# Two gate projections in front of the retention core, swapped output banks, and rotary angles between the first splits

## What is computed

```python
def hybrid_layer(x, positions, ...):
    h = rmsnorm(x, norm_mix)
    cb, cc, cu, q, k, v, g, ga, gb = split(h @ w_in)
    y_conv = short_conv_mixer(cb, cc, cu, conv_w, w_conv_out)
    y_ret = retention_mixer(q, k, v, g, positions, ret_norm, w_ret_out)
    merged = sigmoid(ga) * y_conv + sigmoid(gb) * y_ret
    x = x + merged @ w_o
    h2 = rmsnorm(x, norm_mlp)
    return x + square(relu(h2 @ w_up)) @ w_down

# retention_mixer: 4 heads, q and k of 128, v of 256 features each
q, k = rotary(q, positions) * 128 ** -0.5, rotary(k, positions)
o = retention_core(q, k, v)          # sum over earlier tokens, weights decay with distance
o = (o - mean(o)) * rsqrt(var(o) + EPS) * ret_norm       # mean and variance per head
return (silu(g) * o) @ w_ret_out
```

## Time and profile before

| | |
|---|---|
| median of 3 runs | 2580.82 us (2580.22 to 2585.51) |
| the profiled execution: time, span | 2584.02 us, 2582.0 us |
| TensorE busy with matmuls | 2475.8 us, 96% |
| VectorE, GpSimd, ScalarE busy | 51%, 53%, 31% |
| share of the chain that ended last | TensorE 85%, VectorE 8% and its queue 3% |

### The profile page before, as it was taken

One profiled execution on the slowest core, in us unless ns is written; L12 is line 12 of the kernel. 1 busy time (PEld: TensorE's weight loads), 2 busy tenths in 40 slices (PEclk: granted clock), 3 DMA queues, 4 the chain that ended last, 5 costly groups with the idle time before them and its releaser, 6 DMA issues.

```text
span 2582.0 us, 33584 instructions
## 1 busy us (share of the span) xinstructions
PE 2475.8 (96%) x11384; PEld 2016.4 (78%) x11384; DVE 1306.1 (51%) x1877; ACT 794.7 (31%) x1031; POOL 1369.5 (53%) x1668
## 2 busy tenths in 40 slices
PE   6899999999999998999999999999699998899999
PEld 5677888888888887778888888887477776688887
DVE  7764243345544558722433545545855654532323
ACT  4132212231111221322122311112367774332222
POOL 5425566656666653355665566665023324455554
PEclk9999999999999999999999999999699999999999
DMA  4213323343444332133333442443011111232322
GB/s 162 82 33 97 98 93 94 97 147 98 138 147 139 98 91 64 56 99 96 94 95 98 147 139 97 146 138 116 20 48 58 50 41 56 78 103 94 98 90 97
DMA packets 64450, 247.39 MB, mean 96 GB/s; under 512 B 7152, under 2 KB 9584, under 8 KB 63088
## 3 DMA queue, kind: packets, MB, share of 16 engines
q1 hardware_dynamic: 62064, 218.92, 26.8%
q10 hardware_dynamic: 2304, 27.38, 2.7%
HBM read 244.17 MB, written 2.10 MB: 95 GB/s over the span
## 4 chain that ended last, share of the span: by engine, by line
PE 85%; DVE 8%; DVEq 3%; issue 2%; ACT 1%; DMA 0%; POOL 0%; ACTq 0%; POOLq 0%
PE ps L475 80%; PE ps L712 1%; PE ps L725 1%; DVEq L1316 1%; DVEq L1343 1%; PE ps L741 1%; PE ps L680 1%; DVE H_lo_f L1516 1%; DVE C_lo L1167 1%; DVE A_lo_f L1318 0%; DVE C_lo_f L1351 0%; DVE C_hi_f L1314 0%; DVE C_hi L1165 0%; DVE B_hi_f L1348 0%; DVE C_hi_f L1313 0%
## 5 line engine op out<-in xcount | busy, mean ns | idle before, releaser
L427 POOL TENSOR_TENSOR w_lo<-w_raw,w_hi 128x256 fp32r<-128x256 f32 x1616 | 1339.9, 861 | 1175.5 <-ACT w_hi L884 1044.7
L475 PE MATMUL ps<-H_hi,w_hi 128*128 128x512 f32 x1952 | 779.2, 399 | 16.2 <-DVE H_lo L1522 14.2
L475 PE MATMUL ps<-H_hi,w_lo 128*128 128x512 f32 x1952 | 764.7, 392 | 0.0
L475 PE MATMUL ps<-H_lo,w_hi 128*128 128x512 f32 x1952 | 764.5, 392 | 0.0
L884 ACT ACTIVATE w_hi<-w_raw 128x1024 fp32r<-128x1024 f32 x401 | 422.3, 1056 | 1022.3 <-PE ps L475 982.2
L475 PEld LDWEIGHTS ps<-H_hi,w_hi 128*128 128x128 f32 x1952 | 369.3, 189 | 108.3 <-issue 25.9
L475 PEld LDWEIGHTS ps<-H_hi,w_lo 128*128 128x128 f32 x1952 | 369.2, 189 | 78.6
L475 PEld LDWEIGHTS ps<-H_lo,w_hi 128*128 128x128 f32 x1952 | 369.7, 189 | 77.7 <-issue 4.1
L475 PE MATMUL ps<-A_hi,w_hi 128*128 128x512 f32 x560 | 220.4, 394 | 2.7 <-POOL w_lo L427 2.7
L475 PE MATMUL ps<-A_lo,w_hi 128*128 128x512 f32 x560 | 219.1, 391 | 0.0
L475 PE MATMUL ps<-A_hi,w_lo 128*128 128x512 f32 x560 | 218.9, 391 | 0.0
(11 more groups left out here) (228 smaller groups left out, 2876.5 us busy)
## 6 DMA issues: line engine op xcount, KB each, us to landing
w_raw<-weights SPq DMA_DIRECT2D x404, 512.0 KB, 3.5
mod_w<-mod_weights ACTq DMA_DIRECT2D x8, 3072.0 KB, 10.9
X<-x SPq DMA_DIRECT2D x4, 512.0 KB, 8.2
out<-X SPq DMA_DIRECT2D x8, 256.0 KB, 2.0
toeplitz<-biases SPq DMA_DIRECT2D x14, 128.0 KB, 2.3
decay_sb<-decay ACTq DMA_DIRECT2D x1, 1024.0 KB, 6.1
ctx_sb<-context SPq DMA_DIRECT2D x1, 1024.0 KB, 5.6
mask_sb<-key_mask ACTq DMA_DIRECT2D x1, 320.0 KB, 2.7
```

The source lines that it names most:

```text
L427: last = nc.gpsimd.tensor_tensor(w_lo[:, q, c:c + LOW_COLS], w_raw[:, q, c:c + LOW_COLS], w_hi[:, q, c:c + LOW_COLS].bitcast(F32), ALU.sub ...
L475: mm = nc.tensor.matmul(dst, w[l], xs[r], start=start and a == 0, stop=stop and a == 2)
```

## The change

- `JOB_G` 0 is issued ahead of scores 0 and `JOB_G` 1 behind scores 1; scores 2, which shares bank 1 with gate 1, waits until VectorE has read it. Gates 2 and 3 stand before and behind the last variance, gates 4 to 7 behind the last root.
- `O_BANKS` = (2, 6): heads 0 and 2 now use banks 2 and 3.
- VectorE reads gates 0 and 1 to a new buffer `early` ahead of the core; ScalarE takes their sigmoids there, then does the heads. Its other gate work is unrolled.
- The query and key weights alternate (q0, k0, q1, ...), and scores of head h wait for 2(h+1) tiles only. VectorE's rotary loop is unrolled.
- In layer 0 the angles are divided: cosine after two low parts of H, sine after four, both ahead of the sum of squares. The second half of the value jobs waits for ScalarE's root (`rt_ready`) instead of `rstd_ready`, and in layer 1 also for `mod_read`, as bank 5 held other sums.
- The first split to C_hi, which shares memory with ST, waits until all values are done.

```diff
-        O_BANKS = (6, 2)
+        O_BANKS = (2, 6)
...
                     if i == 1:
-                        pe.wait_ge(rstd_ready, L + 1)
+                        pe.wait_ge(rt_ready, 2 * L + 1)
+                        if L:
+                            pe.wait_ge(mod_read, L)
...
-            def attention(L):
-                pe.wait_ge(tiles_ready, L * LAYER_TILES + TILE_OG)
+            def attention(L, n):
+
+                def g_job(m):
+                    job(n + JOB_G + m, m % RING, H_hi, H_lo, L * LAYER_TILES + TILE_H)
 
                 def scores(u):
                     h, j = divmod(u, TOK)
+                    if j == 0:
+                        pe.wait_ge(tiles_ready, L * LAYER_TILES + TILE_QK + 2 * (h + 1))
+                    if u == 2:
+                        pe.wait_ge(bank_free, n + JOB_G + EARLY_G + RING)
...
                 units = RH * TOK
+                g_job(0)
                 scores(0)
                 scores(1)
+                g_job(1)
                 for u in range(units):
                     if u + 2 < units:
                         scores(u + 2)
                     values(u)
                     if u % TOK == 1 and u > TOK:
                         variance(u // TOK - 1)
+                pe.wait_ge(o_copied, L * RH + (RH - 1))
+                g_job(2)
                 variance(RH - 1)
+                g_job(3)
+                pe.wait_ge(dev_ready, L * RH + RH)
+                for m in range(4, G_JOBS):
+                    g_job(m)
...
-                attention(L)
-
-                jobs(n + JOB_G, G_JOBS, H_hi, H_lo, tiles + TILE_H, before=(dev_ready, L * RH + RH))
+                attention(L, n)
...
                 phase(r + JOB_V // RING + 1, (V_JOBS + QK_JOBS) // RING - 1)
+                for m in range(EARLY_G):
+                    ahead(r + JOB_G // RING, m)
+                    gate(r + JOB_G // RING, m, early[:, m, :], early[:, EARLY_G + m, :])
                 for h in range(RH):
...
-                phase(r + JOB_G // RING, G_JOBS // RING,
-                      lambda r, i, s: gate(r, s, Bf[:, s, :], Bf[:, 4 + s % 2, :]))
+                for m in range(EARLY_G, G_JOBS):
+                    ahead(r + (JOB_G + m) // RING, m % RING)
+                    gate(r + (JOB_G + m) // RING, m % RING, Bf[:, m % RING, :], Bf[:, 4 + m % 2, :])
...
             dve.wait_ge(par_loaded, 32)
-            for m in range(DT):
-                stream_low(0, m, lambda m: column(PAR_NORM1 + m, 0))
...
+            stream_low(0, 0, first_gain)
+            stream_low(0, 1, first_gain)
+            rope_angles(0)
+            stream_low(0, 2, first_gain)
+            stream_low(0, 3, first_gain)
+            rope_angles(1)
+            stream_low(0, 4, first_gain)
+            stream_low(0, 5, first_gain)
             dve.wait_ge(x_squared, 2)
             pair_sum(0, 0, 2)
+            stream_low(0, 6, first_gain)
+            stream_low(0, 7, first_gain)
             dve.wait_ge(x_squared, X_PARTS)
             pair_sum(4, 4, 6)
...
-                with dve.Fori(0, QK_JOBS // RING) as i:
+                for i in range(QK_JOBS // RING):
...
+                for m in range(EARLY_G):
+                    gate_in(r + JOB_G // RING, m, early[:, m, :])
...
-                        gate_in(r + JOB_G // RING + i, q, Bf[:, q, :])
+                        raw, gate = Bf[:, q, :], Bf[:, 4 + q % 2, :]
+                        if m < EARLY_G:
+                            raw, gate = early[:, m, :], early[:, EARLY_G + m, :]
+                        else:
+                            gate_in(r + JOB_G // RING + i, q, raw)
...
+                        if m == 0:
+                            dve.wait_ge(pv_done, (L + 1) * (RH * TOK))
                         split(Clf[:, m, :], C_hi[:, m, :], C_lo[:, m, :])
```

More of the change, by code:

```diff
@@ L62 @@
 JOB_MIX = JOB_CONV + CONV_JOBS
+EARLY_G = 2
 JOB_O = JOB_MIX + PAIR_JOBS
@@ L219, in build @@
         token_rstd = at("token_rstd", 211 * KB, [2 * TOK])
+        early = at("early", 212 * KB, [2 * EARLY_G, S])
         turns = at("turns", 128 * KB, [2, S])
@@ L296, in build @@
         sq_done = sem("sq_done")
-        rstd_ready = sem("rstd_ready")
+        mod_read = sem("mod_read")
         ctx_loaded = sem("ctx_loaded")
@@ L486, in job, with jobs @@
                 mm.then_inc(jobs_done, 1)
-            def jobs(n0, count, hi, lo, tiles, kt=DT, before=None):
+            def jobs(n0, count, hi, lo, tiles, kt=DT):
                 with pe.Fori(0, count // RING) as i:
                     for q in range(RING):
-                        if before is not None and q == 0:
-                            pe.wait_ge(*before)
                         job(n0 + i * RING + q, q, hi, lo, tiles, kt)
@@ L1216, in invert_root @@
                 if by_token:
-                    V.tensor_tensor(rstd_sq[:, :], rstd[:, :], rstd[:, :], ALU.mult).then_inc(rstd_ready, 1)
+                    V.tensor_tensor(rstd_sq[:, :], rstd[:, :], rstd[:, :], ALU.mult)
             V.memset(ones[:, :], 1.0)
@@ L1228, in add_square @@
                 return V.tensor_tensor(E[:, SUMSQ, :], E[:, SUMSQ, :], Hf[:, m, :], ALU.add)
-            dve.wait_ge(par_loaded, 32)
-            for m in range(DT):
-                stream_low(0, m, lambda m: column(PAR_NORM1 + m, 0))
[L1235 to L1263, removed]
@@ L1264, in _, with rope_angles @@
-            pair_sum = lambda dst, a, b: V.tensor_tensor(Af[:, dst:dst + 2, :], Af[:, a:a + 2, :], Af[:, b:b + 2, :], ALU.add)
+            def rope_angles(which):
+                if which == 0:
+                    V.tensor_copy(Cf[:, 0, :], z_pos[:, :])
+                    fence()
+                    V.tensor_scalar(Cf[:, 0, :], Cf[:, 0, :], par[:, PAR_FREQ:PAR_FREQ + 1], None, ALU.mult)
+                shift = (0.25, 0.0)[which]
+                fence()
+                V.tensor_scalar(Cf[:, 1, :], Cf[:, 0, :], INV_2PI, shift, ALU.mult, ALU.add)
+                fence()
+                V.tensor_scalar(Cf[:, 1, :], Cf[:, 1, :], ROUND_MAGIC, None, ALU.add)
+                fence()
+                V.tensor_scalar(Cf[:, 1, :], Cf[:, 1, :], -ROUND_MAGIC, None, ALU.add)
+                fence()
+                V.scalar_tensor_tensor(out=Cf[:, 2, :], in0=Cf[:, 1, :], scalar=-TWO_PI_1, in1=Cf[:, 0, :],
+                                       op0=ALU.mult, op1=ALU.add)
+                fence()
+                V.scalar_tensor_tensor(out=Cf[:, 3, :], in0=Cf[:, 1, :], scalar=-TWO_PI_2, in1=Cf[:, 2, :],
+                                       op0=ALU.mult, op1=ALU.add)
+                fence()
+                V.scalar_tensor_tensor(out=Cf[:, 2, :], in0=Cf[:, 1, :], scalar=-TWO_PI_3, in1=Cf[:, 3, :],
+                                       op0=ALU.mult, op1=ALU.add)
+                fence()
+                if which == 0:
+                    V.tensor_scalar(Cf[:, 2, :], Cf[:, 2, :], HALF_PI, None, ALU.add)
+                    fence()
+                V.tensor_scalar(Cf[:, 4 + which, :], Cf[:, 2, :], PI_LOW, -PI_LOW, ALU.min, ALU.max)
+                if which == 1:
+                    fence()
+                    V.tensor_scalar(Cf[P // 2:P, 5, :], Cf[P // 2:P, 5, :], -1.0, None, ALU.mult).then_inc(angles_ready, 1)
@@ new lines, in _ @@
+            pair_sum = lambda dst, a, b: V.tensor_tensor(Af[:, dst:dst + 2, :], Af[:, a:a + 2, :], Af[:, b:b + 2, :], ALU.add)
+            first_gain = lambda m: column(PAR_NORM1 + m, 0)
+            dve.wait_ge(par_loaded, 32)
+            stream_low(0, 0, first_gain)
[6 more added lines that the diff above has]
+            stream_low(0, 5, first_gain)
@@ L1307, in _, with gate_in @@
                 dve.wait_ge(decay_loaded, 16)
-                with dve.Fori(0, QK_JOBS // RING) as i:
+                def gate_in(r, q, dst):
+                    job_done(r, q)
+                    V.tensor_tensor(dst, ps[:, q, :], rstd[:, :], ALU.mult).then_inc(bank_free, 1)
+                for i in range(QK_JOBS // RING):
                     for q in range(RING):
@@ L1347, in _ @@
                         fence()
-                        V.tensor_tensor(Bf[:, 6, :], Bf[:, q, :], Bf[:, 6, :], ALU.mult)
+                        V.tensor_tensor(Bf[:, 6, :], raw, Bf[:, 6, :], ALU.mult)
                         fence()
                         dve.wait_ge(ev_ready, L * EV_LAYER + (EV_G + m + 1))
-                        V.tensor_tensor(Clf[:, m, :], Bf[:, 4 + q % 2, :], Bf[:, 6, :], ALU.mult)
+                        V.tensor_tensor(Clf[:, m, :], gate, Bf[:, 6, :], ALU.mult)
+                        if m == 0:
+                            dve.wait_ge(pv_done, (L + 1) * (RH * TOK))
                         split(Clf[:, m, :], C_hi[:, m, :], C_lo[:, m, :])
@@ L1468, in _ @@
                 V.tensor_tensor(mod_ctx[:, bass.ds(lanes, 2 * DT)], ps[:, MOD_BANK, 2 * MOD_LAYER:2 * MOD_LAYER + 2 * DT],
-                                par[:, bass.ds(lanes + PAR_BCTX, 2 * DT)], ALU.add)
```

(1 more changed line is left out.)

8 lines of the change are left out of this document (2 added, 6 removed).

## The result

The median after is 2561.4 us (4 runs, 2560.3 to 2562.2), before 2580.6 (4 runs, 2580.2 to 2585.5). The ratio is 0.9921, interval 0.9904 to 0.9938: 19.3 us faster, against a forecast of 22.3. The profiled execution took 2562.2 us, its span is 2560.4 and its mean clock 0.983. Executions of one kernel differ by a few us, so the profile of before (2584.0, 3.4 over its median) isn't as typical of its kernel as that of after (0.8 over).

The account below looks back on a forecast made before the run. TensorE was taken as the bound nearly everywhere, VectorE as setting the gate stage's end. Layer gains -14.2 and -11.4, start +2.3, clock 2 x 0.5 sum to -22.3: 2580.8 to 2558.5 us; own case 2554 to 2563, with rival 1 to 2568.

Parts of the forecast that it names:

- The gate part: Gates moved around the core: query/key end to last-C restart 91.2 us per layer; gains of 14.2 and 11.4 us.
- VectorE's chain without the stop: Behind the core, VectorE goes on at once after the first reciprocal (3.4 us) with two tiles (7.0), instead of idling 12.9.
- The wait for C_lo: TensorE's wait for the last C_lo in the gate stage: 4.6 us instead of 3.5.
- the gate read: TensorE's short wait before scores 2 until VectorE has read bank 1: about 0.8 us.
- VectorE's idle time for gate 1: VectorE, done with its rotary stage and gate 0, waits for gate 1 ahead of the core: 2.0 us.
- T: End of the query/key jobs, before: 115.12 and 1005.36; values were to start at T + 14.8, plus 0.3 for GpSimd.
- the last three reciprocals and six tiles: End of VectorE's chain in the gate stage, taken over unchanged from the kernel before: 41.4 us.
- rival 1: The break at the core drops the clock, 2.3 us a layer; gain 13 to 18, 2563 to 2568; chance 0.17.
- the core's clock was under 1.00: Stated sign that the prediction is wrong: a granted clock in the core under 1.00.
- The start: Layer 0: angles ahead of the sum of squares make TensorE wait 9.3 us; cost +2.3 us, bounds +0.7 to +7.0.
- Rival 5: At the start VectorE waits out whole GpSimd pieces, 1.09 us a step: 15.6 us dearer, 2574; chance 0.02.
- Rival 2: Weights become the bound in the gate stage through ScalarE's casts; 12 us late loses 8 a layer, 2574; chance 0.05.

Follow-up runs that it names:

- start only: The kernel before with the second value half waiting for the root and the angles placed between the first splits; 2582.5 us, ratio 1.0006.
- old banks: The change with `O_BANKS` back at (6, 2), so that gate 2 waits for head 3's copy; 2568.5 us, ratio 0.9943.
- wait only: The kernel before with the second value half waiting for the root instead of `rstd_ready`, angles still behind the sum of squares; 2575.1 us.
- sum first: The change with the eight low parts and the sum of squares ahead of both angles, root wait kept; 2553.1 us, ratio 0.9884.
- gates only: The change with the start and `rstd_ready` of the kernel before; 2560.6 us, ratio 0.9913.
- reciprocal in the core: The sum first kernel with the first reciprocal moved on VectorE from behind the core to ahead of unit 12; 2555.4 us, ratio 0.9898.
- break filled: The change with seven extra 512-column matmuls, their result unread, between scores 2 and the first values; 2561.3 us, ratio 0.9920.
- one gate: The change with only gate 0 ahead of the core, gate 1 behind it ahead of gate 2; 2580.8 us, ratio 0.9993.

## Why the prediction was right

**The gate part** was the gain, and its mechanism held step by step. From the end of the query/key jobs (now 116.2 and 995.8: scores 2 less its wait and the 12.1 us of jobs) to the last-C restart it took 93.8 and 92.5 us, where 91.2 was forecast and 105.3 and 102.7 measured before. So the layers gained 11.5 and 10.2 there, where the sum had 14.2 and 11.4. Of this, 0.9 and 0.4 us were lost again behind the two restarts (forecast 0.5 each), and with the start's 1.1 (forecast 2.3) that makes the 19.3. VectorE's chain without the stop is confirmed by the reciprocals, 10.4 us apart against the forecast 10.4 (3.4 + 7.0). The wait for C_lo was 4.8 (forecast 4.6), for the gate read 0.8 (0.8), VectorE's idle time for gate 1 2.0 (2.0).

Part of this agreement is luck. The 14.2 of layer 0 took the slow first gate of one profiled execution (clock 0.71, stop of 12.9 us) as the kernel's own. In the profile of "start only", whose gate stage is that of the kernel before, layer 0 stops for 10.1 us, as layer 1 does:

```profile
167.98 0.69 DVE L1345 TENSOR_TENSOR B_hi_f<-ps,rstd 128x512 f32<-128x512 f32 x1 [10.14 <-PE ps L475]
```

Against such an execution layer 0 gains some 2.7 us less. The sum was taken off a median (2580.8) although its rows come from an execution of 2584.0.

**What was short** is above all the core of layer 0. Values start at T + 15.4, not + 15.1: GpSimd was busy for 2.69 of the 3.29 us around scores 2, a split of ST took 1.05 us instead of 0.69, and TensorE's wait was 1.88 instead of 1.5. From the values to the first reciprocal it took 25.8 us, 1.5 more than before (128.26 to 152.55), which is the loss of 5 us at clock 0.66 (1.7); the last three reciprocals and six tiles took 42.2 instead of 41.4 (42.5 in layer 1). Most of that lies between the second and the third reciprocal, 14.0 instead of 13.3 in both layers: GpSimd was busy beside VectorE for 10.1 us of that stretch, before for 6.4. The sum had taken this part over unchanged. In layer 0 the drop of rival 1 happened, at 1.7 us instead of its 2.3, and in layer 1 it didn't. The text had also said that it would be wrong if the core's clock was under 1.00; it was, over 5 us, and the sum could bear it. No row of before tells that layer 1 would have 1.00; at 0.50 it would have lost some 2.7 us, as the section on the hardware shows.

**The start** was priced at +2.3 and cost 1.1 in the trace (116.2 against 115.1); "start only" gives +1.8 in the medians, with no change inside its interval. Other profiles with the same start have the end of the query/key jobs at 116.1 to 117.0. The mis-sized term is the sum of squares, ready at 35.4 instead of 36.4. About half of that is the cast of the positions, which started at 10.21, ahead of GpSimd's first piece (10.40), and took 0.42 us; the other half is the sine angle, as GpSimd was done at 26.0 and not at 27.8. E waited 9.0 us (forecast 9.3). The clock's loss, 0.17 x 15.45 = 2.6 us, was near the 3.0 forecast.

**Rival 5** did not occur. The angle steps took 0.79 and 1.07 us beside GpSimd, as in the earlier trace rows, and no step waited out a piece. (The trace has 18 such steps, ten for the cosine and eight for the sine, not the 22 of that rival's sum.) By the Trainium skill, "SBUF — State Buffer", section "Who interferes with whom", the later of two contending operations is blocked wholly; this case's trace doesn't agree, with 0.36 to 0.38 us more per step beside pieces of 15.57 / 16 = 0.97 us.

**Rival 2** did not occur in the change, but the experiments show how near it was. The prediction said that gate 5's weight is split by about 171 and that later ones come 4 to 7 us early. In the change GpSimd ended that split at 171.9. With the old banks, or with gate 1 behind the core, head 3's root comes some 3 us later and gate work stands behind it: VectorE then waits for sigmoids, and by the medians 7 or 19 us are lost. I had seen the swap as worth the 2.2 us wait and its clock, and not ScalarE's queue behind the root.

What stays open: what sets the clock of the core's first 5 us, and why the second block, which no edit touches, took from 775.2 us (the change) to 779.3 (wait only) among these profiles; old banks with its 778.5 lies within that. The unrolled loops of ScalarE and VectorE were part of every kernel with the gate part and were not tested alone.

## What to carry to other kernels

When a job is pulled ahead of a latency-bound stage, look at each in-order queue behind it: here the gain hung on ScalarE having its sigmoids and casts out of the way before a root that waits on TensorE, and 8.7 us of wait appeared from moving one job of 5.4 us. Split an edit whose parts can have opposite signs: the start edit measured as nothing, since it held a gain of 5.5 us and a loss of 7.4, and keeping the good half gave the fastest kernel. A wait taken away ahead of an engine with little slack comes back at its next hand-over (9.8 us sooner became 6.4). And before two profiles are laid side by side, see where their executions lie among all times of their kernels: here the profile of before was 3.4 us over its median, and that of sum first 5.6.

## What the runs showed of the hardware

- Behind the same two waits (0.8 and 1.9 us around small matmuls) the granted clock in the core's first 5 us was 0.66 in layer 0 and 1.00 in layer 1 of the change, 0.50 and 1.00 with gates only, 1.00 and 0.70 with the old banks, and 0.50, all of it at 1.2 GHz, in layer 1 of sum first and of the reciprocal in the core. So the same waits were followed by values from one level to the other. With the second wait filled by matmuls it was 1.00 in both layers. Gates only, layer 0; sum first, both layers; old banks, layer 0:

```profile
128.72:133.72 5.00, 5.00 (x15) 4.43 (x16) 3.20 (x9) 0.00 (x0) 0.00 (x0) 0.50 0.38 105
122.92:127.92 5.00, 5.00 (x15) 4.43 (x16) 3.60 (x9) 0.00 (x0) 2.44 (x3) 0.50 0.26 73
1003.78:1008.78 5.00, 5.00 (x15) 4.42 (x16) 3.19 (x9) 0.00 (x0) 0.00 (x0) 0.50 0.28 105
131.92:136.92 5.00, 5.00 (x30) 4.59 (x30) 4.23 (x11) 0.00 (x0) 0.00 (x0) 1.00 0.36 105
```

- What that clock costs can be read from the first values to the first reciprocal, over the same work and behind the same or a filled break: 24.3 us in five layers at 1.00 (the change, gates only, old banks, both of break filled), 25.8 at 0.66 and 25.6 at 0.70, and 27.0 in three at 0.50 (gates only, both of sum first). At 1.2 GHz those first 5 us thus cost the stage 2.7 us.

- ScalarE's change between the root and the sigmoid shows as a row of its own, ACT_TABLE_LOAD, of 1.28 us. In "one gate" one stood on the chain for which VectorE waited.
